# Modulation products on four 32-column strips, four products in one call per attention step

## What is computed

```python
mod     = silu(c)     @ w_mod + b_mod          # (6 x 1024) for x
mod_ctx = silu(c_ctx) @ w_mod + b_mod          # (6 x 1024) for ctx
sh1, sc1, g1, sh2, sc2, g2 = split(mod, 6, axis=-1)
```

## Time and profile before

| what | value |
|---|---|
| median of 3 runs | 2571.85 us (2568.33 to 2574.39) |
| span of the profiled execution, first to last instruction | 2581.4 us |
| PE busy | 2323.8 us (90%) |
| DVE, ACT, POOL busy | 1045.8, 1147.0, 1210.6 us |
| mean granted TensorE clock | 0.940 |
| modulation products, attention stage of the first layer (L1913) | 144 records, 39.1 us busy |

### The profile page before, as it was taken

One profiled execution on the slowest core, in us unless ns is written; L12 is line 12 of the kernel. 1 busy time (PEld: TensorE's weight loads), 2 busy tenths in 40 slices (PEclk: granted clock), 3 DMA queues, 4 the chain that ended last, 5 costly groups with the idle time before them and its releaser, 6 DMA issues. The chain is left out here.

```text
span 2581.4 us, 42120 instructions
## 1 busy us (share of the span) xinstructions
PE 2323.8 (90%) x18060; PEld 2048.2 (79%) x18060; DVE 1045.8 (41%) x2012; ACT 1147.0 (44%) x1618; POOL 1210.6 (47%) x308
## 2 busy tenths in 40 slices
PE   8998989898999999898989899898984877998998
PEld 7997945487999999775549799775864767997997
DVE  2413754233220220565442321146675777222550
ACT  5433432355442543342146443454893554444442
POOL 6773600063875887440007387442320001585784
PEclk9999978989999999997889999999997898999999
DMA  7453502242653655431215265341202112453552
GB/s 255 164 180 111 162 29 70 98 131 77 198 179 122 206 178 170 124 115 50 82 66 180 82 196 184 119 123 49 66 18 66 47 38 67 147 177 117 180 186 92
DMA packets 303654, 316.40 MB, mean 123 GB/s; under 512 B 7833, under 2 KB 295053, under 8 KB 303213
## 3 DMA queue, kind: packets, MB, share of 16 engines
q1 hardware_dynamic: 303469, 313.72, 37.9%
HBM read 311.53 MB, written 2.16 MB: 122 GB/s over the span
## 5 line engine op out<-in xcount | busy, mean ns | idle before, releaser
L368 POOL TENSOR_TENSOR slab_lo<-ring,slab_hi 128x2048 fp32r<-128x2048 f32 (+1 forms) x242 | 1092.4, 4528 | 796.1 <-ACT slab_hi L357 759.4
L357 ACT CAST slab_hi<-ring 128x2048 fp32r<-128x2048 f32 (+1 forms) x242 | 451.4, 1870 | 592.6 <-PE bank L402 262.5
L433 PE MATMUL bank<-ffn_h_hi,slab_hi 128*128 128x256 f32 x1344 | 331.2, 284 | 0.0
L434 PE MATMUL bank<-ffn_h_lo,slab_hi 128*128 128x256 f32 x1344 | 329.7, 283 | 0.0
L433 PEld LDWEIGHTS bank<-ffn_h_hi,slab_hi 128*128 128x128 f32 x1344 | 257.9, 192 | 0.5 <-issue 0.3
L434 PEld LDWEIGHTS bank<-ffn_h_lo,slab_hi 128*128 128x128 f32 x1344 | 258.0, 192 | 0.1
L1532 POOL TENSOR_TENSOR inv_m<-inv_d,const 128x512 f32<-128x512 f32 x24 | 30.6, 1282 | 365.5 <-ACT inv_d L1595 296.6
L400 PE MATMUL bank<-ffn_hidden_hi,slab_hi 128*128 128x256 f32 x704 | 199.3, 283 | 0.0
L401 PE MATMUL bank<-ffn_hidden_lo,slab_hi 128*128 128x256 f32 x704 | 199.2, 283 | 0.0
L402 PE MATMUL bank<-ffn_hidden_hi,slab_lo 128*128 128x256 f32 x704 | 199.2, 283 | 0.0
L438 PE MATMUL bank<-ffn_h_hi,slab_lo 128*128 128x256 f32 x1344 | 189.0, 283 | 4.4 <-POOL slab_lo L368 4.4
(11 more groups left out here) (642 smaller groups left out, 5785.8 us busy)
## 6 DMA issues: line engine op xcount, KB each, us to landing
ring<-in_ffn_w_in SPq DMA_DIRECT2D x88, 1024.0 KB, 5.1
ring<-in_ffn_w_out SPq DMA_DIRECT2D x32, 1024.0 KB, 5.0
ring<-in_w_in SPq DMA_DIRECT2D x30, 1024.0 KB, 5.3
ring<-in_mix_w_in SPq DMA_DIRECT2D x24, 1024.0 KB, 5.3
ring<-in_w_mod SPq DMA_DIRECT2D x24, 1024.0 KB, 5.2
ring<-in_w_up SPq DMA_DIRECT2D x22, 1024.0 KB, 5.1
ring<-in_ffn_w_out SPq DMA_DIRECT2D x16, 768.0 KB, 4.3
ring<-in_mix_w_out SPq DMA_DIRECT2D x8, 1024.0 KB, 5.1
```

The costliest lines, as they stand in the source:

```text
L357: act.copy(self.hi[i % self.PLACES][:, 0:w], K.ring[n % RING][:, 0:w]).then_inc(self.hi_ready, 1)
L368: pool.tensor_tensor(self.lo[i % self.PLACES][:, 0:w], place[:, 0:w], self.hi[i % self.PLACES][:, 0:w].bitcast(F32), ALU.subtract).then_in ...
L433: pe.matmul(out, w[0][:, k, col], act[0][:, k, :], start=(k == 0), stop=False)
L434: pe.matmul(out, w[0][:, k, col], act[1][:, k, :], start=False, stop=False)
```

## The change

`K.cs` is widened from 2 to 32 columns, 30 of them zeros (one more memset at the start). The product of k-tile k writes a strip of 32 PSUM partitions, strip k mod 4, and so uses 32 columns of the array; each strip adds up two of a slab's eight products. `mod_rows` becomes 128 x 3072, and a copy 128 x 256. The 24 transposes at the end become 24 products: 128 x 128 of `mod_rows` as the stationary operand, and `modsum`, a 128 x 2 selector with ones in row c of each strip, as the moving one; they add the four parts and turn them at once. A call is now four products, and there is one call in a step, between the scores and the scan part, in place of three of two products. Ahead of the attention stand four calls of four in place of eight of two.

```diff
+    parts["modsum"] = np.stack([i % 32 == c for c in range(2)], 1)
...
-        self.cs = self.sb("cs", [P, KD, 2])
+        self.cs = self.sb("cs", [P, KD, 32])
...
+        dve.memset(self.K.cs[:, :, :], 0.0)
...
-    AT_A_CALL = 2
+    AT_A_CALL = 4
+    STRIPS = 4
     BANKS = (6, 7)
     FIRST = 3
-    AHEAD = 8
+    AHEAD = 4
...
-        self.rows = K.sb("mod_rows", [2, MOD_SLABS * HALF], ctx=ctx)
+        self.rows = K.sb("mod_rows", [P, MOD_SLABS * HALF], ctx=ctx)
...
-        return self.K.bank[n % 2][0:2, HALF * (n // 2):HALF * (n // 2 + 1)]
+    def place(self, n):
+
+        return (self.K.bank[n % 2], HALF * (n // 2)) if n < self.FIRST else (self.K.bank[self.BANKS[n % 2]], 0)
+
+    def product(self, pe, n, k):
+
+        bank, at = self.place(n)
+        strip = k % self.STRIPS
+        return pe.matmul(bank[32 * strip:32 * strip + 32, at:at + HALF], self.K.cs[:, k, :], self.w[:, k, :],
+                         start=(k < self.STRIPS), stop=(k >= KD - self.STRIPS))
...
+    def copy(self, act, n):
+
+        bank, at = self.place(n)
+        act.copy(self.rows[:, n * HALF:(n + 1) * HALF], bank[:, at:at + HALF]).then_inc(self.copied, 1)
...
-            last = pe.matmul(K.bank[self.BANKS[self.n % 2]][0:2, 0:HALF], K.cs[:, self.k, :], self.w[:, self.k, :],
-                             start=(self.k == 0), stop=(self.k == KD - 1))
+            last = self.product(pe, self.n, self.k)
...
-        while self.copies < min(MOD_SLABS, self.FIRST + (self.AHEAD + step * calls) * self.AT_A_CALL // KD):
+        while self.copies < min(MOD_SLABS, self.FIRST + (self.AHEAD + step) * self.AT_A_CALL // KD):
...
-            last = pe.transpose(K.bank[6][:, 2 * t:2 * t + 2], self.rows[:, t * P:(t + 1) * P], K.c("ident", slice(0, 2), n=2))
+            last = pe.matmul(K.bank[6][:, 2 * t:2 * t + 2], self.rows[:, t * P:(t + 1) * P], K.c("modsum"),
+                             start=True, stop=True)
...
-    CALLS = 3
-
-    def pe(self, pe, between=lambda: None, mid_step=lambda i: None):
+    def pe(self, pe, mid_step=lambda i: None):
...
-            between()
             mid_step(i)
...
-            between()
             m = i - 2
...
-            between()
...
-                att.pe(pe, between=lambda: mod.some(pe), mid_step=lambda i: scan.pe(pe, i + EARLY))
+                att.pe(pe, mid_step=lambda i: (mod.some(pe), scan.pe(pe, i + EARLY)))
...
-                att.act(act, at_step=lambda i: (mod.act(act, i, att.CALLS), scan.act(act, i + EARLY - 1)))
-                mod.act(act, KD * MOD_SLABS, 1)
+                att.act(act, at_step=lambda i: (mod.act(act, i), scan.act(act, i + EARLY - 1)))
+                mod.act(act, KD * MOD_SLABS)
```

More of the change, by code:

```diff
@@ L1869 @@
 class Modulations:
-    AT_A_CALL = 2
+    AT_A_CALL = 4
+    STRIPS = 4
     BANKS = (6, 7)
     FIRST = 3
-    AHEAD = 8
+    AHEAD = 4
     def __init__(self, K, ctx):
         self.K, self.n0, self.k, self.n, self.copies = K, K.eaten, 0, 0, 0
-        self.rows = K.sb("mod_rows", [2, MOD_SLABS * HALF], ctx=ctx)
+        self.rows = K.sb("mod_rows", [P, MOD_SLABS * HALF], ctx=ctx)
         self.copied, self.turned, self.kept = K.sem("mod_copied"), K.sem("mod_turned"), K.sem("mod_kept")
-    def first_place(self, n):
-        return self.K.bank[n % 2][0:2, HALF * (n // 2):HALF * (n // 2 + 1)]
+    def place(self, n):
[5 more added lines that the diff above has]
+                         start=(k < self.STRIPS), stop=(k >= KD - self.STRIPS))
     def pe_first(self, pe):
@@ L1890, in pe_first @@
         for n in range(self.FIRST):
-            w = view(K.next_slab(pe))
+            self.w = view(K.next_slab(pe))
             for k in range(KD):
-                last = pe.matmul(self.first_place(n), K.cs[:, k, :], w[:, k, :], start=(k == 0), stop=(k == KD - 1))
+                last = self.product(pe, n, k)
             K.slab_done(last)
         self.n = self.FIRST
+    def copy(self, act, n):
+        bank, at = self.place(n)
+        act.copy(self.rows[:, n * HALF:(n + 1) * HALF], bank[:, at:at + HALF]).then_inc(self.copied, 1)
     def act_first(self, act):
-        K = self.K
-        K.wait_slabs(act, self.n0 + self.FIRST)
+        self.K.wait_slabs(act, self.n0 + self.FIRST)
         for n in range(self.FIRST):
-            act.copy(self.rows[:, n * HALF:(n + 1) * HALF], self.first_place(n)).then_inc(self.copied, 1)
+            self.copy(act, n)
         self.copies = self.FIRST
@@ L1918, in some, with act @@
                 self.k, self.n = 0, self.n + 1
-    def act(self, act, step, calls):
-        K = self.K
-        while self.copies < min(MOD_SLABS, self.FIRST + (self.AHEAD + step * calls) * self.AT_A_CALL // KD):
[L1924 to L1927, removed]
+    def act(self, act, step):
+        while self.copies < min(MOD_SLABS, self.FIRST + (self.AHEAD + step) * self.AT_A_CALL // KD):
+            self.K.wait_slabs(act, self.n0 + self.copies + 1)
+            self.copy(act, self.copies)
+            self.copies += 1
     def pe_end(self, pe):
```

## The result

| | before | after |
|---|---|---|
| median of 4 runs | 2570.93 us (2568.33 to 2574.39) | 2594.88 us (2583.68 to 2601.71) |
| ratio, 95% interval | 1 | 1.0085 (1.0059 to 1.0112) |
| profiled execution, span | 2581.4 us | 2599.6 us |
| mean granted clock | 0.940 | 0.912 |

The change makes the kernel slower, by 24 us in the medians. I had forecast 2555 us. The time lies 0.9 us outside my range, and on the side to which I gave 0.32. The scatter of the runs goes with the clock too: of 28 more runs of the kernel before, the fastest (2559.61 us) has a mean granted clock of 0.953, the slowest (2589.64 us) 0.939.

The account below looks back on a forecast made before the run. TensorE was taken to bound the kernel (90% busy). Calls -23.2, selector +7.6, inversion +1.6 and half-clock stretch +5.0 gave -9.0 in layer 1, -8.2 in layer 2; from 2571.85 us this gave 2555, range 2538 to 2594.

Parts of the forecast that it names:

- the side to which I gave 0.32: Whole kernel: chance 0.32 that the change makes it slower.
- two in steps 0 and 1 at half clock: Attention steps 0 and 1: two four-product calls at half clock cost 1.9 us, with full clock back by step 2.
- eight calls in steps 2 to 9 cost 8 x 0.53: Attention steps 2 to 9: eight four-product calls at full clock cost 4.2 us a layer.
- The clock stays down: Rival, from step 0 on: clock fails to rise, +25 us a layer, 2580 us (one) or 2605 (both); chance 0.30.
- at the high clock PE is busy for all of them: Argument against the clock staying down: steps 2 to 9 hold no wait, so PE is busy throughout.
- one layer: Upper range: clock stays down in one layer only, 2580 us, plus part of the two-layer case, up to 2594.
- the call: Modulation call of eight records on four strips running abreast: 0.53 us at full clock, 0.95 at half.
- the selector: End of the stage: 48 records at half clock take 10.3 us in place of 2.72, +7.6 a layer.
- the inversion: Ahead of the attention, after PE idles before 388: inversion takes 3.68 us against 2.08, +1.6 (0 to 2).
- the two waits for VectorE: Ahead of the attention: shorter bursts leave PE idle some 8 us before 388 and over 5 before 417.
- the stretch behind the second one: From 417 to 427 us: runs at half clock after the idle wait, +5.0 us (0 to 6.3).
- the slack of the scan chain: Attention steps: 3.3 us between VectorE's state update and PE's read shrinks to 0.9, but holds.

Follow-up runs that it names:

- The run on one strip: The change with all eight products of a slab written to strip 0, none side by side: 2573.57 us, ratio 0.9983 to the kernel before.
- two products of zeros a call: The change with slabs 0 to 5 on one strip, six calls ahead, and two zero products added to each step call: 2564.54 us, ratio 0.9949.
- confirmed alone: The kernel before with only its 24 transposes replaced by 24 fp32 products: 2582.92 us, ratio 1.0032.
- one strip ahead: The change with slabs 0 to 4 on one strip and slabs 5 to 11 on four: 2590.46 us, ratio 1.0073.
- With one a call: The change with slabs 0 to 5 on one strip, six calls ahead, and one zero product in each step call: 2568.66 us, ratio 0.9973.
- real products on two strips: The change with slabs 0 to 5 on one strip, slabs 6 to 11 on two, nothing added: 2563.55 us, ratio 0.9973.

## Why the prediction was wrong

*The step that failed* is the return of the clock, "two in steps 0 and 1 at half clock", "eight calls in steps 2 to 9 cost 8 x 0.53". Of those eight calls, five ran at half clock (steps 2 and 4 to 7), and with them most of the other work of these steps: steps 0 to 9 got 5.7 us shorter in layer 1 in place of 24.1, and that is 18.4 of the 19.6 us between the forecast's -9.0 for the layer and the measured +10.6. The rival "The clock stays down" had this mechanism, its place and its price; I gave it 0.30 and the forecast 0.40. Its price was 25 us a layer, 2605 for both layers. The measured 2594.9 is lower because the clock was back from 456 to 462 and for steps 8 and 9 from 497 on.

*Why I chose wrongly.* Against the rival I had written that "at the high clock PE is busy for all of them". The row from 463 to 496 shows what that is worth: busy for 33.00 of 33 and at 0.50. I judged by idleness, from the two lengths of the inversion. The run on one strip shows that products abreast don't hold the clock as the same products in line do, and the one with two products of zeros a call that more products in line hold it. And the range should have reached to both layers: nothing in the mechanism differs between the two, so "one layer" was no case to stop at.

*Right:* the call (0.57 for 0.53, at half clock 1.01 for 0.95), so strips do run abreast; the selector (10.40 for 10.3), confirmed alone; the inversion (+1.6); the two waits for VectorE (9.23 and 4.35 for 8 and over 5); the stretch behind the second one (14.6 us from L2144 to the first scores, before 9.8, so +4.8 for +5.0); the slack of the scan chain, which holds even at full clock, as the waits of the kernel with two zeros show; copies and loads at nothing. The rest of the forecast's sum can be checked only roughly: with the clock held by two products of zeros a call, the stage of layer 1 takes 142.3 us (376.86 to 519.13) against 153.0 before, and 12 x 0.86 = 10.3 us of that are zeros. That kernel also has half the slabs on one strip and steps 0 and 1 at full clock, so it isn't the forecast's kernel.

*The two rules of the Trainium skill.* The section "Loop structure matters more than you think" of the page "TensorE: Matmul & The Clock Gate" of the Trainium skill names idle gaps as what lets the clock fall. The trace agrees for the pauses ahead (an inversion of 3.68 us for 2.08), but the worse loss had no gap at all. The section "LDWEIGHTS (loading the stationary operand)" of the same page of the Trainium skill makes a load its columns divided by 1.2 GHz, by which the selector would take 48 x 0.107 = 5.1 us, an estimate. It took 10.40, with 128 rows as with two.

## What to carry to other kernels

Ask of any saving on TensorE what the clock does next: a product that ran in hidden or spare time may be what keeps the others at full speed, and a change that shortens it can lose more than it saves. A busy PE is not a fast PE; read the granted clock of every stretch beside the busy share. Before packing products, look for short waits that precede a fall of the clock and put existing work there: here that alone gave 0.6% (interval 0.3 to 0.8), with no new operation.

## What the runs showed of the hardware

- At full clock eight records on four 32-column strips take 0.57 us, on two 0.98, on one 1.85: 0.43, 0.86 and 1.72 for two, four and eight records of 0.215 in line, and about 0.13 more each.
- The granted clock can stay at 0.50 with PE busy and waiting for nobody: 33.00 of 33 us in the kernel after, 70.00 of 70 with one strip ahead. The same list of instructions ran at 0.50 in most steps with the products side by side on four strips, and at 1.00 with them one after another on one.
- Products of zeros help to hold the clock: with two a call it stayed at 1.00 for 112 us where it was 0.50 from 456 to 489 without them. With one a call the ratio is that of real products on two strips, calls of the same length (0.9973 both).
- An fp32 product with 128 stationary columns and two streamed ones takes 0.217 a record at half clock (10.40/48) with 2 rows or 128, and 0.118 at full (2.83/24); an fp32 transpose with the same stationary operand takes 0.113 at half clock (2.72/24) and is one record where the product is two. So replacing a small transpose by a product costs nearly four times as much here (10.40 for 2.72).
